# Layer borders: the last three output units by token parts instead of two, a ring of 15 squares, and the last sum inside the next first unit

## What is computed

```python
def rms_norm(x, g):
    xf = x.astype(jnp.float32)
    y = xf * lax.rsqrt(jnp.mean(xf * xf, axis=-1, keepdims=True) + NORM_EPS)
    return (y * g.astype(jnp.float32)).astype(x.dtype)
...
for i in range(DEPTH):
    hp = rms_norm(xp, norm_pre[i])
    ...
    yp, _ = mixer_a(hp, ...)        # or b, or c; each ends in "(...) @ w_out"
    ...
    xp = xp + rms_norm(yp, norm_post[i])
```

## Time and profile before

| | |
|---|---|
| median of 3 runs | 2428.85 us (2426.31 to 2430.08) |
| the profiled execution | 2424.72 us, of which the span of the core 2422.9 us |
| TensorE busy | 2357.7 us, 97% of the span |
| VectorE, ScalarE, GpSimd busy | 1222.1, 887.0, 91.5 us |
| mean granted clock of TensorE | 0.990 of full speed |
| first part-wise piece of the last pair, A to B | starts at 774.16 us |
| the same, B to C | 1225.29 us |
| the same, C to A | 1585.93 us |
| the same, last layer | 2377.85 us |

### The profile page before, as it was taken

The page is one execution under the profiler, slowest core; times in us unless marked ns, Lnnn a source line. Parts: engine busy times, 40 slices in busy tenths (PEclk is TensorE's granted clock), DMA queues, the critical chain, the costliest instruction groups (busy, mean ns, idle before and its releaser), DMA issues.

```text
span 2422.9 us, 34821 instructions
## 1 busy us (share of the span) xinstructions
PE 2357.7 (97%) x14951; PEld 2281.7 (94%) x14951; DVE 1222.1 (50%) x1741; ACT 887.0 (37%) x1254; POOL 91.5 (4%) x44
## 2 busy tenths in 40 slices
PE   8999999999999989998999989999999999999996
PEld 7999999999999888886899989999999999999996
DVE  4444454454333746657257867365444454545235
ACT  5323332233232524455352356253324223323221
POOL 0000000000000002222000011000000000000000
PEclk9999999999999999999999999999999999999998
DMA  3111111111121421111222111322111111111213
GB/s 135 44 44 44 44 44 44 36 44 44 63 70 53 143 83 53 45 45 36 105 82 70 44 35 44 116 82 78 52 44 44 44 36 44 44 44 41 91 45 105
DMA packets 58489, 145.79 MB, mean 60 GB/s; under 512 B 8904, under 2 KB 29528, under 8 KB 58328
## 3 DMA queue, kind: packets, MB, share of 16 engines
q1 hardware_dynamic: 53056, 135.34, 17.4%
q10 hardware_dynamic: 5280, 8.22, 1.3%
HBM read 121.47 MB, written 18.37 MB: 58 GB/s over the span
## 4 chain that ended last, share of the span: by engine, by line
PE 85%; DVE 8%; ACT 3%; DVEq 2%; ACTq 2%; issue 1%; DMA 0%; POOL 0%
PE ps L502 61%; PE ps L526 6%; PE ps L733 4%; PE ps L583 3%; PE ps L646 2%; PE ps L594 2%; PE ps L639 1%; PE ps L775 1%; PE ps L883 1%; PE ps L750 1%; PE ps L761 1%; PE ps L786 1%; DVE l_hs L1854 1%; DVE x L1368 1%; DVE w_lo L1329 1%
## 5 line engine op out<-in xcount | busy, mean ns | idle before, releaser
L502 PE MATMUL ps<-l_h_hi,w_hi 128*128 128x344 f32 x2448 | 526.3, 323 | 0.0
L502 PE MATMUL ps<-l_h_lo,w_hi 128*128 128x344 f32 x2448 | 520.1, 321 | 0.0
L502 PE MATMUL ps<-l_h_hi,w_lo 128*128 128x344 f32 x2448 | 517.0, 319 | 0.0
L502 PEld LDWEIGHTS ps<-l_h_lo,w_hi 128*128 128x128 f32 x2448 | 414.3, 189 | 0.0
L502 PEld LDWEIGHTS ps<-l_h_hi,w_hi 128*128 128x128 f32 x2448 | 409.8, 188 | 1.2
L502 PEld LDWEIGHTS ps<-l_h_hi,w_lo 128*128 128x128 f32 x2448 | 408.2, 188 | 0.0
L1329 DVE TENSOR_TENSOR w_lo<-w_raw,w_hi 128x1024 fp32r<-128x1024 f32 x182 | 229.7, 1263 | 274.1 <-ACT w_hi L920 265.0
L920 ACT ACTIVATE w_hi<-w_raw 128x1024 fp32r<-128x1024 f32 x182 | 190.8, 1049 | 125.3 <-DMA w_raw<-in_wu 99.8
L1436 DVE TENSOR_TENSOR l_tmp<-ps,rx 128x1032 f32<-128x1032 f32 x64 | 78.9, 1233 | 287.5 <-PE ps L502 287.3
L502 PE MATMUL ps<-l_y_lo,w_hi 128*128 128x344 f32 x912 | 193.5, 320 | 0.0
L502 PE MATMUL ps<-l_y_hi,w_hi 128*128 128x344 f32 x804 | 171.3, 321 | 0.4 <-DVEq L1868 0.4
(11 more groups left out here) (238 smaller groups left out, 3622.3 us busy)
## 6 DMA issues: line engine op xcount, KB each, us to landing
w_raw<-in_wu SPq DMA_DIRECT2D x182, 512.0 KB, 3.5
x_save<-x SPq DMA_DIRECT2D x9, 1376.0 KB, 5.4
x<-x_save SPq DMA_DIRECT2D x21, 516.0 KB, 6.7
l_sw<-l_q ACTq DMA_DIRECT2D x32, 129.0 KB, 2.7
out_y<-x SPq DMA_DIRECT2D x6, 688.0 KB, 3.4
x<-in_xt SPq DMA_DIRECT2D x4, 688.0 KB, 10.4
x<-in_xt SPq DMA_DIRECT2D x5, 516.0 KB, 6.2
x<-in_xt ACTq DMA_DIRECT2D x3, 516.0 KB, 3.6
```

What stands on the lines that cost most here:

```text
L502: mm = nc.tensor.matmul(ps[:, 3 * slot + ch, 0:CW], wt[:, w, k, :], mv[:, k, ch * CW:(ch + 1) * CW], start=(k == 0 and t == 0), stop=(k == ...
```

## The change

- `LAST` goes from `KT - 2` to `KT - 3`: whole output units 5 instead of 6, and `last_pair` becomes `last_triple`: (0,0), (1,0), (2,0), (0,1), [sum 0], (1,1), (2,1), (0,2), [sum 1], (1,2), (2,2). The three units use slots 1, 0, 1 (`triple_slot`), so a piece of unit 2 waits for the read-out of the same part of unit 0. The squares of units 0 and 1 both go through one buffer `sq_own` and are added by VectorE one by one; those of unit 2 go to `rx`.
- `results_at_end` follows: the weight of the next layer's first unit can be loaded when (0,2) is computed, its second when (1,2), its third when (2,2) is.
- The ring of squares has 15 places: 9 in `L.squares`, in a region where the new layer will write its results later, 3 in `sq_ring`, 3 in `sqt`.
- `post(prev, 2)` moves from behind the second unit's part 0 to behind the fourth k-step of the first unit's part 0.
- The hand-written orders in both `cross` functions are new. In particular the last output unit's weight halves and the next layer's first two weights stand elsewhere.

```diff
@@
-LAST = KT - 2
-SQ_RING = 6
+LAST = KT - 3
+SQ_RING = 15
@@
-        def square_place(c, k):
+        def square_place(L, c, k):
             s_ = (KT * c + k) % SQ_RING
-            return sq_ring[:, s_, :] if s_ < CH else sqt[:, part(s_ - CH)]
+            if s_ < 9:
+                return L.squares[:, s_ // CH, part(s_ % CH)]
+            return sq_ring[:, s_ - 9, :] if s_ < 12 else sqt[:, part(s_ - 12)]
@@
-                results_at_end.append(3 * n + 3 if u not in (L.u0, L.u1 - 2) else 3 * n + 5)
+                results_at_end.append(3 * n + (7 if u == L.u1 - 3 else 5 if u in (L.u0, L.u1 - 2) else 3))
@@ TensorE
-                pe.wait_ge(*L.yssq_done.at(LAST + c + 1))
-                pe.wait_ge(*L.ysq_done.at(LAST + 2 * c + 2))
+                pe.wait_ge(*L.yssq_done.at(LAST + 2 * c + 2))
+                pe.wait_ge(*L.ysq_done.at(LAST + 3 * c + 3))
@@
+            def last_triple(L, hi, lo):
+                u, r = L.u1 - 3, L.r1 - 3
                 def piece(j, c):
+                    slot = triple_slot(j)
                     if c == 0:
                         pe.wait_ge(w_lo_done, u + j + 1)
-                    pe.wait_ge(evac[j], 3 * (r // 2) - 2 + c)
-                    piece_of(j, u + j, c, hi, lo).then_inc(result, 1)
+                    pe.wait_ge(evac[slot], 3 * (r // 2) + 2 * c + 1 if j == 2 else 3 * ((r + j) // 2))
+                    piece_of(slot, u + j, c, hi, lo).then_inc(result, 1)
                 piece(0, 0)
                 piece(1, 0)
+                piece(2, 0)
                 piece(0, 1)
                 post(L, 0)
                 piece(1, 1)
+                piece(2, 1)
                 piece(0, 2)
                 post(L, 1)
                 piece(1, 2)
+                piece(2, 2)
@@ first_pair, part 0
                             square_sum(k, 0)
+                            if k == 3 and prev is not None:
+                                post(prev, 2)
                         pe.wait_ge(w_lo_done, u + 2)
                         for k in range(KT):
                             mm = products(1, k, 0)
                         mm.then_inc(result, 1)
-                        if prev is not None:
-                            post(prev, 2)
@@ ScalarE, cross: the new order behind out_squares(0, 1)
+                    root_post(0)
+                    h_tiles(0, range(0, 2))
+                    out_squares(1, 1)
+                    h_tiles(0, range(2, 4))
+                    out_squares(2, 1)
+                    h_tiles(0, range(4, 7))
+                    out_squares(0, 2)
+                    root_post(1)
+                    h_tiles(0, range(7, KT))
+                    h_tiles(1, range(0, 1))
+                    next_weight(0)
+                    out_squares(1, 2)
+                    h_tiles(1, range(1, 3))
+                    out_squares(2, 2)
+                    next_weight(1)
+                    h_tiles(1, range(3, 7))
+                    root_post(2)
@@ VectorE, cross: the new order behind out_sum(0, 1); out_add does something in layers A only
+                    tiles(0, range(0, 2))
+                    out_add(1, 1)
+                    out_sum(1, 1)
+                    tiles(0, range(2, 4))
+                    out_add(2, 1)
+                    tiles(0, range(4, 6))
+                    out_add(0, 2)
+                    tiles(0, range(6, KT))
+                    out_sum(0, 2)
+                    tiles(1, range(0, 2))
+                    next_weight(0)
+                    out_add(1, 2)
+                    out_sum(1, 2)
+                    tiles(1, range(2, 4))
+                    out_add(2, 2)
+                    next_weight(1)
+                tiles(1, range(0 if prev is None else 4, KT))
```

More of the change, by code:

```diff
@@ L173, in s @@
                 return Signal(shared[name], before)
+            L.squares = at(n + "squares", O_AT + (0 if i and layers[-1].kind == "a" else KT * TILE), [P, 3, NT])
             L.h_hi = at(n + "h_hi", H_AT, [P, KT, NT], F32R)
@@ L593, in square_sum @@
                             pe.wait_ge(*L.root.at(1))
[L594 removed]
+                    mm = nc.tensor.matmul(ps[:, 7 - c % 2, 0:CW], ones[:, :], square_place(L, c, k), start=(k == 0), stop=(k == KT - 1))
                     mm.then_inc(*((L.ssq_mm.sem, 1) if k == KT - 1 else (L.sq_used.sem, 1)))
@@ L695, in layer_a @@
                 units(LAST, u, r, *second, lambda k: L.y_low.at(KT + k + 1))
-                last_pair(L, *second)
+                last_triple(L, *second)
             class Tiles:
@@ L930, in out_squares @@
                     else:
[L931 to L935, removed]
+                        act.wait_ge(result, triple_done(prev, j, c))
+                        src = ps[:, 3 * slot + c, 0:CW]
+                    if j < 2:
+                        act.wait_ge(*prev.yssq_done.at(LAST + 2 * c + j))
+                    nc.scalar.activation(rx[:, part(c)] if j == 2 else sq_own[:, :], src, ACT.Square).then_inc(prev.ysq_done.sem, 1)
                     if prev.kind != "a":
-                        nc.scalar.activation(prev.acc[:, LAST + j, part(c)], src, ACT.Copy).then_inc(evac[j], 1)
-                    elif j == 1:
+                        nc.scalar.activation(prev.acc[:, LAST + j, part(c)], src, ACT.Copy).then_inc(evac[slot], 1)
+                    elif j == 2:
                         act.dma_start(x[:, 2:2 + A_EARLY, part(c)], prev.saved.rearrange("k p n -> p k n")[:, 2:2 + A_EARLY, part(c)]
@@ L1334, in out_add, with out_sum @@
                 def out_add(j, c):
[L1336 to L1339, removed]
-                    V.drain().then_inc(prev.acc_done.sem, 1)
-                def out_sum(c):
-                    dve.wait_ge(*prev.ysq_done.at(LAST + 2 * c + 1))
-                    V.tensor_tensor(ssq[:, part(c)], ssq[:, part(c)], sqt[:, part(c)], ALU.add).then_inc(prev.yssq_done.sem, 1)
+                    if prev.kind == "a":
+                        slot = triple_slot(j)
+                        dve.wait_ge(result, triple_done(prev, j, c))
+                        acc = prev.acc[:, LAST + j, part(c)]
+                        V.tensor_tensor(acc, ps[:, 3 * slot + c, 0:CW], acc, ALU.add)
+                        V.drain().then_inc(evac[slot], 1)
+                        V.drain().then_inc(prev.acc_done.sem, 1)
+                def out_sum(j, c):
+                    dve.wait_ge(*prev.ysq_done.at(LAST + 3 * c + j + 1))
+                    V.tensor_tensor(ssq[:, part(c)], ssq[:, part(c)], sq_own[:, :], ALU.add).then_inc(prev.yssq_done.sem, 1)
+                    V.drain()
                 def low(c, k):
@@ L1392, in cross, with next_weight @@
                 else:
[L1393 to L1416 removed]
+                    def next_weight(j):
+                        if L is not None:
+                            w_low(L.u0 + j)
+                    out_add(0, 0)
+                    w_low(prev.u1 - 1)
+                    out_sum(0, 0)
+                    out_add(1, 0)
+                    out_sum(1, 0)
+                    out_add(2, 0)
+                    out_add(0, 1)
+                    out_sum(0, 1)
+                    tiles(0, range(0, 2))
+                    out_add(1, 1)
[6 more added lines that the diff above has]
+                    out_sum(0, 2)
+                    tiles(1, range(0, 2))
+                    next_weight(0)
[5 more added lines that the diff above has]
+                tiles(1, range(0 if prev is None else 4, KT))
                 if L is not None:
```

72 lines of the change are left out of this document (22 added, 50 removed).

## The result

The changed kernel takes **2433.27 us** (median of 16 runs, 2430.22 to 2435.96), the kernel before beside it 2428.44 (16 runs, 2424.68 to 2432.15): ratio 1.002, 95% interval 1.0013 to 1.0028, so 3.2 to 6.8 us slower. The forecast was 2433.3. The profiled execution took 2432.5 us, its span is 2430.7.

What follows compares the result with a forecast made beforehand. TensorE, busy 97% of the span, was taken as the bound. A to B +1.7, the other borders +3.2 and clock +2.2, end -2.7 gave +4.4 us: 2433.3 us against the median, range 2429.3 to 2437.

Steps and rivals of the forecast that it cites:

- The first weight is late: Next layer's first unit: TensorE waits for the weight's low half, 3.5 us at A to B, 2.3 at B to C and C to A.
- Rival 1: At the borders the first weight comes in time and the change does what its parts promise: 2421.2 us, chance 0.1.
- The old wait goes: First square sum of part 1: the waits for the root, 1.84 us at A to B and twice 0.7, go.
- The moved sum waits 1.6 us at A to B and not elsewhere: At `post(prev, 2)`, TensorE waits 1.6 us for its inputs at A to B, not at B to C.
- That the slow clock covers it: At A to B the clock falls, 1.7 us as before, and now covers the moved sum's 1.6 us wait.
- rival 3: A further wait: late load, uncovered 1.6 us at the moved sum, or second slow stretch; 2436.6 us, chance 0.1.
- The clock at the plain borders: At B to C and C to A the clock's fall costs 4/6 x 1.7 = 1.1 us each.
- The ring of 15 at nothing: ScalarE's short waits for TensorE's square sums go, but ScalarE has slack there: 0 us.
- The end, -2.7: Behind TensorE's last piece VectorE has 13.4 to 13.6 us left instead of 16.3: gain 2.7 us (2.5 to 3.0).
- The sum: Borders and end together: +1.7 at A to B, +3.2 and clock +2.2 at the others, end -2.7, making +4.4 us.

Runs made afterwards that it cites:

- experiment 4: `reordered`: changed kernel, same work in another order on ScalarE and VectorE, `post(prev, 2)` behind the second unit's fourth k-step; 2421.91 us, ratio 0.9971 to the kernel before.
- sum_late: Changed kernel with `post(prev, 2)` back behind the second unit's part 0; 2434.94 us, ratio 1.0028 to the kernel before.
- ring9: Changed kernel with a ring of 9 places for the squares in place of 15; 2434.6 us, ratio 1.0021 to the kernel before.
- weight_early: Changed kernel with the next layer's first weight moved earlier in ScalarE's and VectorE's queues; 2432.0 us, ratio 1.0006 to the kernel before.
- changed_again: Changed kernel run once more, unaltered, for a second profile; 2434.88 us, ratio 1.0028 to the kernel before.
- experiment 5: Kernel before with only `post(prev, 2)` moved behind the first unit's fourth k-step; 2444.33 us, ratio 1.0065 to the kernel before.
- reordered_sum_first: The kernel of experiment 4 with `post(prev, 2)` behind the first unit's fourth k-step; 2437.5 us, ratio 1.0034 to the kernel before.

## Why the prediction was right

The time was 2433.3 against 2433.27, closer than its terms were. Step by step:

- **The first weight is late** (3.5, 2.3, 2.3 us): right, 3.30, 1.99 and 2.01. In the chain at B to C each stage stood within 0.4 us of its count, from the start of (0,0) at 1219.13: load issued at 27.8 (27.8 counted), high half 36.1 (36.3), low half done 38.4 (38.65). Rival 1 needed it done before 36.3 and fell; experiment 4 shows that another order gets there. The count was 0.2 to 0.3 us long at each border.
- **The old wait goes**: right, none at L610. But sum_late, with the sum in its old place, has only 0.35 us of it at each border: the moved sum takes away no more than that, and the rest goes by the new order and, at A to B, by the late weight.
- **The moved sum waits 1.6 us at A to B and not elsewhere**: right, 1.42, and the add of (2,2) at 808.45 - 764.10 = 44.35 (44.5 counted). **That the slow clock covers it** held in the second profile and in that of ring9 and not in the first, with 55.8 or 55.9 us in all three: A to B came out at +1.54 and +1.56 (+1.7 forecast). I had named it as a cost of its own in rival 3; here it was an either-or, and no extra. Where the fall comes behind the sum, as in weight_early, both are paid.
- **The clock at the plain borders** (1.1 us each, from 4 falls in 6): somewhat dear. In the four profiles with this wait unchanged (changed, changed_again, ring9, sum_late) it fell at 4 of 8, at 1.6 us: 0.8 each. With 1.32 us for the waits that makes +4.2 for the two borders, +5.4 forecast.
- **The ring of 15 at nothing**: right in the new order (9 places do as well); in the old one it gives 0.3 us at each plain border. That the new order cannot do with fewer than 9 the prediction did not say.
- **The end, -2.7**: mechanism right, size 2.2 to 2.4. From the last piece's end (2414.85 - 1.88 = 2412.97) to the last update it is 13.9 us (13.4 to 13.6 counted), as VectorE's last rows show: the tiles of x that a transfer brings back were waited for 0.85 us where I had allowed 0.5.

```profile
2413.54 0.51 DVE L1360 TENSOR_TENSOR l_acc<-ps,l_acc 128x344 f32<-128x344 f32 x1
...
2419.08 0.87 DVE L1388 TENSOR_TENSOR l_acc<-l_acc,rx 128x688 f32<-128x688 f32 x1 [0.85 <-DMA x<-x_save]
...
2425.80 1.06 DVE L1391 SCALAR_TENSOR_TENSOR x<-l_acc,g_post,x 128x344 f32<-128x344 f32 x2
```

- **The sum**: +4.4 forecast, 3.5 and 3.6 found at the places that it speaks of. The medians say 4.8 and 4.9; the remaining 1.3 us lie inside the measurement's interval (3.2 to 6.8) and are put down to nothing. So the hit to a tenth is partly luck: the plain borders were 1.2 us too dear, 1.3 us lie outside the sum, and the kernel before came out 0.4 us under the median that I added to.

## What to carry to other kernels

When more units are kept in hand at once, ask first what they hold: here three units filled the ring of three weight buffers, so the next load could start 28 us later in the border, and the conversion behind it then had to find a place in two busy queues. (A ring of four, by which the load would not wait for these three units, was not run; that the order alone takes the wait away is shown by `reordered`.) A transfer can be early and its consumer late: look for idle time ahead of the instruction that reads it (here 2.37 us on ScalarE, one tile before the weight), and for what stands in front of it on its engine. An instruction moved earlier is only as early as its last input; count the place that it goes to as carefully as the one that it leaves (3.2 us saved, 13.8 spent in experiment 5). And compare stretch by stretch, since one profile can differ from another by some us in stretches that nothing touched: layer B, the same in all ten, took 396.9 to 403.2 us.

## What the runs showed of the hardware

- Whether TensorE's granted clock falls from 2.4 to 1.2 GHz behind an idle stretch is not set by its length alone: 1.99 and 2.01 us were followed by a fall in 4 of 8 cases, 3.30 in 3 of 4 (not in the first profile: 803.80:820.00 at 1.00), the 1.84 us at A to B in both profiles that have them, 1.55 and 1.57 (weight_early) in neither case, 2.25 and 2.26 (reordered_sum_first) in both. The Trainium skill, TensorE: Matmul & The Clock Gate, Part 1: The HAM clock gate (the "warmup" mystery), calls the ramp at a kernel's start variable from run to run; these rows show the like at waits in mid-kernel.
- A wait costs more than its idle time. B to C without a wait is 50.56 us (reordered); with one it is 52.84 - 1.99 = 50.85 or 51.18 - 0.35 = 50.83, and A to B with two is 55.80 - 4.72 = 51.08. So some 0.27 us come on top of each, and the rows show them in two pieces. The first matmul behind a wait takes 0.43 in place of 0.32 us. And matmuls without a wait start 0.16 us apart (799.13 and 799.29 in experiment 4) though each row is 0.32 long, so idle time counted from the end of a row is 0.16 short. Together that is 0.27.
- At the program's start TensorE's matmuls take longer for a time that differs between profiles: of the first two units' products (L599, L583) 7 fall into 10.5 to 14 us in both profiles of the changed kernel, 11 in those of before and of the pair with a ring of 15. The clock row says 1.00 in all of them. Over all kernels these two units take 37.2 to 38.7 us. What sets it was not tried, and whether the changed kernel's 7 twice is chance is open.
